# SBUF buffers of a four-block float32 network on multiples of 128 bytes

## What is computed

```python
for i in range(DEPTH):                       # DEPTH = 2
    x = x + 0.5 * swiglu(rms_norm(x, ffn1_norm[i]), ffn1_w_gate[i], ffn1_w_up[i], ffn1_w_down[i])
    h = rms_norm(x, mix_norm[i])
    x = x + (even_mixer if i % 2 == 0 else odd_mixer)(h, ...)
    x = x + 0.5 * swiglu(rms_norm(x, ffn2_norm[i]), ffn2_w_gate[i], ffn2_w_up[i], ffn2_w_down[i])

def swiglu(x, w_gate, w_up, w_down):         # 1024 -> 2816 -> 1024
    return (jax.nn.silu(x @ w_gate) * (x @ w_up)) @ w_down
```

## Time and profile before

| what | value |
|---|---|
| median of three executions | 1933.03 us (1932.16 to 1934.13) |
| the profiled execution, its own time | 1935.95 us |
| its span, first to last instruction | 1934.2 us |
| around the span | 1.75 us |
| TensorE busy (matmul) | 1891.3 us, 98% of the span |
| VectorE busy | 1464.2 us, 76% |
| ScalarE busy | 1021.2 us, 53% |
| mean granted TensorE clock | 0.995 of full |

### The profile page before, as it was taken

How to read it: one execution, slowest core, us unless ns; L and a number is a source line. 1 busy time by engine, 2 the same in 40 slices (tenths; PEclk the granted TensorE clock), 3 DMA queues, 4 the chain that set the end, 5 groups by cost and what they waited for, 6 DMA issues and landing times.

```text
span 1934.2 us, 31514 instructions
## 1 busy us (share of the span) xinstructions
PE 1891.3 (98%) x11934; PEld 1677.0 (87%) x11934; DVE 1464.2 (76%) x2329; ACT 1021.2 (53%) x1638; POOL 193.3 (10%) x251
## 2 busy tenths in 40 slices
PE   7999999999999999999999999999999999999998
PEld 5989889788878989898898999977778779999897
DVE  8858848767679859767985876756989868769585
ACT  6625525477776526345662643554555766436252
POOL 1121100000001101100010110011111001101010
PEclk9999999999999999999999999999999999999999
DMA  7746673321136646543574654267765377557341
GB/s 232 201 137 167 141 157 91 115 77 55 55 120 177 161 131 185 153 123 116 149 186 120 173 143 139 65 159 173 165 142 131 89 203 189 148 151 188 116 123 60
DMA packets 94661, 271.17 MB, mean 140 GB/s; under 512 B 10568, under 2 KB 10824, under 8 KB 94512
## 3 DMA queue, kind: packets, MB, share of 16 engines
q1 hardware_dynamic: 63456, 201.22, 30.6%
q0 software_dynamic: 29232, 64.50, 19.4%
q10 hardware_dynamic: 1824, 3.44, 1.1%
HBM read 223.07 MB, written 2.28 MB: 117 GB/s over the span
## 4 chain that ended last, share of the span: by engine, by line
PE 83%; DVE 10%; ACT 3%; issue 2%; DMA 1%; ACTq 0%; DVEq 0%
PE ps_unit L795 12%; PE ps_unit L796 12%; PE ps_unit L797 12%; PE ps_y L859 6%; PE ps_y L861 6%; PE ps_y L860 6%; PE ps_s L859 4%; PE ps_s L861 4%; PE ps_s L860 4%; PE ps_t L859 4%; PE ps_t L861 3%; PE ps_t L860 3%; PE ps_s L795 1%; DVE cv L2440 1%; PE ps_s L796 1%
## 5 line engine op out<-in xcount | busy, mean ns | idle before, releaser
L1396 ACT ACTIVATE gw_hi<-gu 128x512 fp32r<-128x512 f32 (+1 forms) x400 | 318.9, 799 | 151.5 <-PE ps_s L861 70.5
L1923 DVE TENSOR_TENSOR gw_lo<-gu,gw_hi 128x512 fp32r<-128x512 f32 (+1 forms) x400 | 355.2, 901 | 55.9 <-ACT gw_hi L1396 42.0
L795 PE MATMUL ps_unit<-a_hi,w_hi 128*128 128x512 f32 x892 | 353.0, 396 | 11.2 <-DVE w_lo L1851 8.8
L796 PE MATMUL ps_unit<-a_lo,w_hi 128*128 128x512 f32 x892 | 349.4, 392 | 0.0
L797 PE MATMUL ps_unit<-a_hi,w_lo 128*128 128x512 f32 x845 | 330.8, 391 | 0.0
L1328 ACT ACTIVATE w_hi<-raw 128x1024 fp32r<-128x1024 f32 (+1 forms) x125 | 125.2, 1003 | 322.9 <-PE ps_unit L797 316.9
L795 PEld LDWEIGHTS ps_unit<-a_hi,w_hi 128*128 128x128 f32 x892 | 168.7, 189 | 50.6 <-DVE w_lo L1851 11.5
L2056 DVE TENSOR_TENSOR t<-ps_unit,half 128x512 f32<-128x512 f32 x96 | 66.3, 691 | 185.8 <-PE ps_unit L797 185.8
L796 PEld LDWEIGHTS ps_unit<-a_lo,w_hi 128*128 128x128 f32 x892 | 168.7, 189 | 33.3
L797 PEld LDWEIGHTS ps_unit<-a_hi,w_lo 128*128 128x128 f32 x845 | 159.6, 189 | 34.2
L859 PE MATMUL ps_y<-xu_hi,gw_hi 128*128 128x256 f32 x640 | 180.4, 282 | 2.3 <-ACT sqb L1400 2.3
(11 more groups left out here) (319 smaller groups left out, 4668.7 us busy)
## 6 DMA issues: line engine op xcount, KB each, us to landing
gu<-gu_stream_dram SPq DMA_DIRECT2D x176, 512.0 KB, 4.8
raw<-w_stream_dram SPq DMA_DIRECT2D x136, 512.0 KB, 3.3
gu<-gu_stream_dram SPq DMA_DIRECT2D x80, 256.0 KB, 3.0
gu<-gu_stream_dram POOLq DMA_DIRECT2D x80, 256.0 KB, 4.2
gu<-gu POOLq DMA_DIRECT2D x80, 256.0 KB, 3.4
w_lo<-raw POOLq DMA_DIRECT2D x28, 512.0 KB, 5.1
raw<-w_stream_dram SPq DMA_DIRECT2D x32, 384.0 KB, 3.0
w_lo_3rd<-raw POOLq DMA_DIRECT2D x15, 512.0 KB, 5.3
```

What stands on the lines that cost most here:

```text
L795: pe.matmul(ps, lhs_hi, rhs_hi, start=first, stop=False)
L796: pe.matmul(ps, lhs_hi, rhs_lo, start=False, stop=False)
L1396: act.activation(gw_hi[:, w, :], src, ACT.Copy).then_inc(gw_hi_done, 1)
L1923: dve.tensor_tensor(gw_lo[:, w, :], src, gw_hi[:, w, :].bitcast(F32), ALU.subtract).then_inc(gw_lo_done, 1)
```

## The change

The helper rounds the next free byte up to a multiple of 128 when the buffer has 512 bytes or more, and the shared stage begins at a multiple of 128:

```diff
         def sb(name, shape, dt=F32, at=None):

             size = int(np.prod(shape[1:])) * 4
+            if at is None and size >= 512:
+                top[0] = (top[0] + 127) // 128 * 128
             if at is None:
                 at, top[0] = top[0], top[0] + (size + 31) // 32 * 32
             return nc.alloc_sbuf_tensor_at(name, shape, dt, offset=at)
...
-        stage = top[0]
+        top[0] = stage = (top[0] + 127) // 128 * 128
```

## The result

The change makes the kernel slower. Six executions of the kernel after give a median of 1950.49 us (1947.71 to 1953.21), against 1933.18 us (1932.16 to 1934.13) for six of the kernel before. The ratio is 1.009, with a 95% interval of 1.008 to 1.010. The profiled execution took 1949.41 us with a span of 1947.3. The forecast of 1910 is wrong in sign; what happened is the slower rival, which I gave 0.06.

A forecast was written before the change was run, and what follows sets the result against it. The prediction took TensorE's operand reading in the hidden tiles as the bound. Terms of 19.2, 0.8, 2.2 and 0.9 summed to 23.1 us, taking the median from 1933.03 to 1910; range 1902 to 1926 us.

The forecast's parts named there:

- the slower rival: Hidden tiles: the operands' distance counts, so xs products lose and xu gains nothing; 1949 to 1959 us, chance 0.06.
- What bounds the kernel: Hidden tiles, 80 in all: TensorE reading its operands sets the pace; it is busy 98% of the span.
- xu to 1.36, 19.2 us: Hidden tiles: all seven products take 1.36 us, 9.52 against 9.76 per tile, 19.2 us less over 80 tiles.
- First tile after a down stage, 0.8 us: Eight places: two xs products each fall from 1.41 to 1.36 us, 0.8 us less.
- Plain tiles, 2.2 us: Eight plain tiles, 48 matmuls of 512 columns each: 11.20 to 10.88 us per tile, 2.2 us less.
- Attention, 0.9 us: 192 matmuls weighing values, 256 moving columns: 5 ns less each at 113.3 ns, 0.9 us less.
- VectorE, ScalarE: Splits of 1024 columns: pace doesn't depend on alignment, worth nothing; VectorE needs 9.36 us a tile, under 9.52.
- DMA at nothing: Loads: only the first, 3.80 us, is on the chain; costed at nothing.
- The estimate of 0.3 us: First DMA wait: 64 beats instead of 70 for a 2048-byte row would take 0.3 us off; left out of the sum.
- The rule on lines: SBUF lines of 16 bytes make starts at 64 and 128 the same; by it alone the time stays at 1933.

The follow-up runs named there:

- kick_2: gap_192 with two extra matmuls of 256 columns ahead of the first hidden tile after each of eight down stages; 1915.96 us, ratio 0.9911.
- pairs: Separate kernel computing nothing of the reference: 30 repeated matmuls per pair of operand starts; at 256 columns 120.0 ns at distance 0, 117.7 at 64, 118.3 at 128.
- stage_64: Kernel after with the shared stage 64 bytes further on, so gw is 64 from xs by 256; 1949.28 us, ratio 1.0075.
- gap_192: Kernel before with xu alone moved to remainder 128 by 256, so xs and xu both lie 192 beyond gw; 1935.6 us, ratio 1.0008.
- xu_64: Kernel before with xu alone moved up by 64 bytes; 1942.6 us, ratio 1.0042.

## Why the prediction was wrong

- **What bounds the kernel: right.** TensorE's pace in the hidden tiles carries over to the time one for one, down (kick_2) and up (after).
- **xu to 1.36, 19.2 us: the step that failed.** I read the 113.3 ns of xs, on a multiple of 128, and the 120 of xu, 64 beyond one, as a property of the moving buffer. It was one of the pair: xs lay 192 from gw, xu 0. The change moves xu and gw together, so their distance stays 0, and xu stays at 120 (excess 16.3 and 16.8). It moves gw away from xs, from 192 to 128, and xs lost what it had: 16.8 us.
- **The evidence that misled me.** I called the down units and the taps the best evidence, and put the slower rival at 0.06 because a and w at distance 0 are the fastest pair of 512 columns. That is so (226.7 ns, in pairs as well), but pairs shows the opposite for 256 columns, where 0 is among the slowest. The taps shift only the moving operand, so they change its place and the distance together and can't tell the two apart. For 256 columns at distance 0 the rows had xu itself, at 120, and the few matmuls of pt with v in rows 5, which I read as 115 and up to 120: neither ran at 113.3.
- **The rival's price.** The slower rival had 16 us at 1.41 and 25.6 at 1.44, 1949 to 1959. 1950.5 came, at its lower end, since xs went to 1.42 and 1.43 from 1.36 and 1.38. Its reason, that only the pair apart was fast, was the right one; only its remainder by 128 was not, for it is the one by 256 that counts (stage_64).
- **First tile after a down stage, 0.8 us.** I took the 1.41 of rows 4 for the weights' remainder. gap_192 has the same 1.41 and the same 1.36 with the same weights; it is the rhythm. After the change these products take 1.44 and 1.45, so the term was a loss.
- **Plain tiles, 2.2 us.** The tile went from 11.20 to 11.15 us. Their distance went from 192 to 128, not to the 0 at which 512 columns take 226.7. The excess over that pace fell by 0.3 us in all.
- **Attention, 0.9 us.** Nothing: its excess over 113.3 is 0.9 us in both kernels. v and pt moved together.
- **VectorE, ScalarE: right.** 1222 ns for 1223. VectorE's wait before its gate, which I expected to fall from 0.40 to 0.16 us, is 0.45 in the slower tile. Whether it covers a tile of 9.52 us is answered by kick_2: TensorE never waits for gw_lo there, only 3.0 us in all, in eight places, for VectorE's `t` (1.7 before).
- **DMA at nothing: right.** The first wait is 3.79 us for 3.80, and the loads of gu land in 4.8 us in both. The estimate of 0.3 us took rows of 2048 bytes; this load has 4096 (512.0 KB on 128 partitions), which would halve it, and the trace shows 0.01.
- **The rule on lines.** By the lines of 16 bytes in the Trainium skill, SBUF — State Buffer, section Door 1: The DMA port swizzle, 64 and 128 are the same start, and the time would have stayed. Pairs disagrees for TensorE's reads: moving starts at 0, 64 and 192 give 120.0, 117.7 and 113.3 ns. The page gives the lines for SBUF and says nothing there of two operands read at once.

What stays open: why these distances and not others, whether gw and xs moved together keep the pace in the kernel as they do in pairs, why 16 and 112 behave otherwise in a repeated pair than in the kernel, and what exactly puts a stream into one rhythm. Two, three and six whole matmuls ahead of the group do it and two of 64 columns don't; other counts, widths and places weren't tried.

## What to carry to other kernels

Alignment of each buffer by itself isn't the quantity for TensorE: look at the start of the moving operand minus that of the weights, by 256, for each pair and each number of columns. Cut a back-to-back stretch at the starts of its products and compare pairs of the same column count only; evidence from 512 columns doesn't carry over to 256. Before trusting a pace, look whether it holds from one group of tiles to the next: an average of 116 ns (gap_192) can be two states, and a few extra matmuls can be worth more than they cost.

## What the runs showed of the hardware that was not expected

- Repeated matmuls of fp32r with 256 moving columns follow each other in 113.3 to 123 ns at full granted clock (2.4 GHz), depending on the distance of their operands by 256 (pairs); at 16 and 192 the same distance has shown more than one pace. At 512 columns it is 226.7 (distance 0) to 236.5 ns (distance 4), at 128 columns about 112 at any of the three that I tried.
- At distance 192 the stream has two paces, 113.3 and 117.8 ns, and stays in one for up to 55 products, 77.7 us, with the other engines and DMAs busy beside it. Two extra matmuls of 256 columns after a down stage change it for the whole group. The same program can begin in either.
- In xu_64 xs stayed in the slow pace beside xu at distance 64 once it was in it, and in the fast one for the first 41 products; in the kernel before, an xs product behind xu at distance 0 went from slow to fast (121, 122, 115, 115, then 113 ns). Moving xu alone cost xs 10.7 us, though the distance of xs stayed as it was.
